# Forming the first of four weight sums of every FFN pair: an accumulating transfer from HBM issued by GpSimd in the place of a VectorE addition

## The chip, the cores and the metric

The kernel runs on one core of a Trainium2 chip. The metric is the device time of one execution in microseconds (us), lower is better. Matmul work runs on TensorE (PE), elementwise work on VectorE (DVE) and ScalarE (ACT), transfers are issued by SyncE (SP), and GpSimd (POOL) computes nothing in this kernel.

## What is computed

Two layers of a hybrid trunk, on 128 context tokens and 512 latent tokens of width 1024 (640 tokens in all), each of the form half-step SwiGLU, token mixing, half-step SwiGLU. The change touches the SwiGLU layers alone, of which there are four (`ffn_w_in` is 1024 x 5632 for each, `D_FF` is 2816):

```python
def _swiglu(h, w_in, w_out):
    g, u = jnp.split(h @ w_in, 2, axis=-1)
    return (jax.nn.silu(g) * u) @ w_out

x = x + 0.5 * mod[:, :, 2] * _swiglu(modulated(0, x), ffn_w_in[l, 0], ffn_w_out[l, 0])
...
x = x + 0.5 * mod[:, :, 8] * _swiglu(modulated(2, x), ffn_w_in[l, 1], ffn_w_out[l, 1])
```

All is float32. The kernel splits each operand in a high part (float32r, ScalarE) and a low part (the difference, VectorE) and makes each product of three matmuls: high x high, high x low, low x high.

## The kernel before, in words

**FFNs and pairs.** The four FFNs are f = 0 to 3. The hidden width of 2816 is worked off in 11 steps d = 0 to 10, each of two 128-column tiles of the gate half and two of the value half; the text calls a step a pair. Step 0 is computed plainly. Steps 1 to 10 use a scheme of seven products of half-size blocks in the place of eight: the weight block of a step is cut into a11 and a21 (input rows 0 to 511; gate columns and value columns) and a12 and a22 (input rows 512 to 1023; gate and value columns), and the seven weight operands ("items" t = 0 to 6) are these blocks or sums and differences of them. An item is 24 matmuls on PE (two parts s = 0, 1 of four k-steps and three products). Every four steps (chunks of 4, 4 and 3: after d = 3, 7 and 10) eight output units of the second weight follow, and x is updated. So steps 4 and 8 start behind output units, and step 1 behind the plain step; the others follow each other directly.

**Raw weights.** `w_raw` has two halves of 1 MB. Half 0 holds a11 and a21 of a step, half 1 holds a12 and a22. SP loads a half by two transfers of 512 KB (`load_in`, L832 to L839; `raw_in[0]` and `raw_in[1]` count the landings). It may load half 0 of step d + 1 once the low part of item 4 of step d is made (`lo_ready`) and the four sums of step d are (`sums_done`); half 1 once the low part of item 6 is. On SP's queue the loads stand between those of `w_mod` ("grains" of 512 KB), four of them ahead of or behind some steps.

**Sums.** `weight_sum(f, d, i)` (L2485) makes four operands in place in `w_raw`, on VectorE, one instruction of 128 x 1024 elements each: i = 0 is a21 = a21 + a22, and waits for both halves; i = 1 is a11 = a21 - a11, i = 2 is a12 = a12 - a11, i = 3 is a12 = a22 - a11. Item 1 is the result of i = 0, so the high part of item 1 (`item_hi`, ScalarE, L1906) waits for `sums_done`; the low part of it (`item_lo`, VectorE, L2476) waits for the high part; and PE waits for the low part (`lo_ready`). High and low parts go to a ring of four slots (`w_hi`, `w_lo`), so that item 1 of step d + 1 may be made once PE is done with item 4 of step d.

**Order.** The order on each engine is written out by hand. On VectorE, in `double(f, d)` (L2783), the first sum and the low part of item 1 of the next step stand in the middle of the step d, and between two additions of step d that PE waits for:

```python
                elif d > 1:
                    weight_sum(f, d + 1, 0)
                for s in range(2):
                    part_done(f, d, 5, s)
                    dve.wait_ge(p5_kept, done + s + 1)
                    dve.tensor_tensor(work[:, s, 2, :], work[:, s, 2, :], role(d, s, "A"), ALU.add).then_inc(c22_done, 1)
                    if not last and d > 1:
                        if s == 0:
                            item_lo(f, d + 1, 1)
```

The addition (L2815) of part s = 1 takes a bank that part s = 1 of item 6 of step d then writes: PE waits for `c22_done` at its start (`free_part`, L1081 to L1084: `t == 6`). For step 2 (`d == 1` in `double`) the first sum and the low part stand behind both additions. For step 1 the first sum stands in `sum_forms` (L2680), for steps 4 and 8 in `lead_step` (L2853), beside the output units.

On ScalarE, `double` (L2116) makes the high part of item 1 of the next step behind the two copies `keep_u2` (L2114); behind it stand two SiLUs (L2142) and the high part of item 2.

## Time and profile before

| | before |
|---|---|
| median of 3 runs | 2393.9 us (2392.03 to 2394.64) |
| the profiled execution | 2396.54 us |
| its span | 2394.7 us |
| PE busy (share of the span) | 2340.2 us (98%) |
| DVE busy | 1568.7 us (66%) |
| ACT busy | 973.1 us (41%) |
| POOL busy | 0.2 us (0%) |
| DMA queue of SP | 249.07 MB, 31.8% of 16 DMA engines' span |

The profile shows one execution. The span is the time from the first to the last instruction; the profiled execution took 1.8 us more than its span. Busy time of PE is the time covered by matmuls; what is missing to the span is idle time of PE, each piece of it put down to the instruction that ended it. A row of a group gives line, engine, operation, out<-in, count, busy time, mean time of one, and the engine's idle time just before them with its releasers. A row of a timeline gives start, duration, engine, line, operation and, in brackets, how long the engine was idle before it and what it waited for.

### The profile page before, as it was taken

How to read it: one execution, taken by the hardware profiler on the slowest of the kernel's cores; microseconds unless marked ns; L12 is line 12 of the kernel's file. 1: busy time of each engine (PE TensorE's matmuls, PEld its weight loads, DVE VectorE, ACT ScalarE, POOL GpSimd, SP SyncE). 2: the span in 40 equal slices, each digit the busy share in tenths (PEclk: the TensorE clock that was granted, in tenths of full speed). 3: DMA queues.
4: the chain of work that ended last, by engine and by line, in shares of the span. 5: the costliest groups of instructions: out<-in, count | busy, mean ns of one | idle time of the engine just before them, and what ended most of it. 6: DMA issues, size and time to landing. Idle time of an engine off the chain costs nothing.

```text
span 2394.7 us, 39770 instructions
## 1 busy us (share of the span) xinstructions
PE 2340.2 (98%) x16652; PEld 2263.6 (95%) x16652; DVE 1568.7 (66%) x2366; ACT 973.1 (41%) x1545; POOL 0.2 (0%) x4
## 2 busy tenths in 40 slices
PE   7999999999989999999999999999999999999999
PEld 6999999989769999999999999999999999999998
DVE  4886776657766876677587767676245768467463
ACT  6533423354556433414374243245215364334142
POOL 0000000000000000000000000000000000000000
PEclk9999999999999999999999999999999999999999
DMA  8342544322101252434224344333221012322132
GB/s 293 124 146 94 193 149 166 132 72 63 47 19 54 89 159 89 141 124 141 89 72 174 108 156 152 115 111 99 88 71 45 19 54 71 106 71 89 53 97 71
DMA packets 201420, 251.61 MB, mean 105 GB/s; under 512 B 12994, under 2 KB 178074, under 8 KB 201242
## 3 DMA queue, kind: packets, MB, share of 16 engines
q1 hardware_dynamic: 201242, 249.07, 31.8%
q8 instruction: 132, 2.16, 0.4%
q14 instruction: 46, 0.38, 0.1%
HBM read 245.76 MB, written 3.28 MB: 104 GB/s over the span
## 4 chain that ended last, share of the span: by engine, by line
PE 84%; DVE 6%; ACT 4%; DMA 3%; issue 3%; SPq 0%; DVEq 0%; ACTq 0%
PE banks L1052 72%; DMA w_raw<-ffn_w_in 2%; DVE w_lo L2476 2%; ACT w_hi L1906 1%; PE banks L1199 1%; DVE w_raw L2497 1%; PE banks L1390 1%; PE banks L1392 1%; PE banks L1391 1%; PE banks L1477 1%; PE banks L1489 1%; DVE hid_lo L2754 1%; ACT prob L2278 0%; PE banks L1504 0%; PE banks L1670 0%
## 5 line engine op out<-in xcount | busy, mean ns | idle before, releaser
L1052 PE MATMUL banks<-b_hi,w_hi 128*128 128x320 f32 x2496 | 779.3, 312 | 15.6 <-DVE b_lo L2654 7.9
L1052 PE MATMUL banks<-b_hi,w_lo 128*128 128x320 f32 x2496 | 772.8, 310 | 0.0
L1052 PE MATMUL banks<-b_lo,w_hi 128*128 128x320 f32 x2496 | 772.8, 310 | 0.0
L1052 PEld LDWEIGHTS banks<-b_hi,w_hi 128*128 128x128 f32 x2496 | 469.9, 188 | 35.3 <-issue 23.2
L1906 ACT ACTIVATE w_hi<-w_raw 128x1024 fp32r<-128x1024 f32 x296 | 310.3, 1055 | 416.8 <-PE banks L1052 235.9
L2476 DVE TENSOR_TENSOR w_lo<-w_raw,w_hi 128x1024 fp32r<-128x1024 f32 x296 | 361.5, 1223 | 171.7 <-ACT w_hi L1906 170.1
L1052 PEld LDWEIGHTS banks<-b_lo,w_hi 128*128 128x128 f32 x2496 | 470.1, 188 | 0.0
L1052 PEld LDWEIGHTS banks<-b_hi,w_lo 128*128 128x128 f32 x2496 | 470.0, 188 | 0.0
L1052 PE MATMUL banks<-hid_hi,w_hi 128*128 128x320 f32 x1664 | 397.0, 311 | 3.0 <-DVE hid_lo L2754 1.5
L1052 PE MATMUL banks<-hid_lo,w_hi 128*128 128x320 f32 x1664 | 394.1, 309 | 0.0
L1052 PE MATMUL banks<-hid_hi,w_lo 128*128 128x320 f32 x1664 | 394.0, 309 | 0.0
L1052 PEld LDWEIGHTS banks<-hid_hi,w_hi 128*128 128x128 f32 x1664 | 281.7, 188 | 4.8 <-DVE hid_lo L2754 2.3
L1052 PEld LDWEIGHTS banks<-hid_hi,w_lo 128*128 128x128 f32 x1664 | 282.1, 188 | 0.0
L1052 PEld LDWEIGHTS banks<-hid_lo,w_hi 128*128 128x128 f32 x1664 | 282.0, 188 | 0.0
L2504 DVE SCALAR_TENSOR_TENSOR x<-banks,mod,x 128x128 f32<-128x128 f32 x354 | 134.9, 433 | 220.9 <-PE banks L1052 220.8
L2497 DVE TENSOR_TENSOR w_raw<-w_raw 128x1024 f32<-128x1024 f32 x160 | 195.3, 1221 | 15.8 <-DMA w_raw<-ffn_w_in 10.2
L1912 ACT ACTIVATE w_hi<-w_raw 128x1024 fp32r<-128x1024 f32 (+1 forms) x96 | 93.3, 984 | 236.4 <-PE banks L1052 236.4
L2085 ACT ACTIVATE hid_hi<-work 128x640 fp32r<-128x640 f32 x88 | 64.2, 733 | 158.8 <-DVE work L2835 149.0
L2482 DVE TENSOR_TENSOR w_lo<-w_raw,w_hi 128x1024 fp32r<-128x1024 f32 (+1 forms) x96 | 107.7, 1132 | 9.8 <-ACT w_hi L1912 9.1
L1895 ACT ACTIVATE w_hi<-w_raw 128x2048 fp32r<-128x2048 f32 (+1 forms) x26 | 48.0, 1846 | 103.4 <-PE banks L1052 49.4
L2805 DVE TENSOR_TENSOR work<-work,banks 128x320 f32<-128x320 f32 x80 | 38.0, 484 | 74.3 <-ACT work L2114 74.3
L2459 DVE TENSOR_TENSOR w_lo<-w_raw,w_hi 128x2048 fp32r<-128x2048 f32 (+1 forms) x24 | 52.8, 2201 | 47.3 <-ACT w_hi L1895 47.3
(326 smaller groups left out, 2550.6 us busy)
## 6 DMA issues: line engine op xcount, KB each, us to landing
w_raw<-ffn_w_in SPq DMA_DIRECT2D x176, 512.0 KB, 4.9
mod_grain<-w_mod SPq DMA_DIRECT2D x84, 512.0 KB, 6.0
w_raw<-ffn_w_out SPq DMA_DIRECT2D x64, 512.0 KB, 4.5
last_grain<-w_mod SPq DMA_DIRECT2D x44, 512.0 KB, 6.0
w_raw<-ffn_w_out SPq DMA_DIRECT2D x32, 384.0 KB, 3.8
w_raw<-w_in_odd SPq DMA_DIRECT2D x20, 512.0 KB, 4.8
mod_first<-w_mod SPq DMA_DIRECT2D x3, 2048.0 KB, 15.8
w_raw<-w_in_even SPq DMA_DIRECT2D x12, 512.0 KB, 5.0
```

The costliest lines, as they stand in the source:

```text
L1052: ins = pe.matmul(o, w3[w], v3[v][cols], start=first and i == 0, stop=last and i == 2, skip_group_check=onto_read)
L1199: ins = pe.matmul(bank[MODB][b * MOD_ROWS:(b + 1) * MOD_ROWS, 0:KIND_COLS], wide_c[:, kt, :], by_features(grain[q])[:, b], start=kt == 0, ...
L1895: act.activation(split_view(w_hi, kind, parity(unit)), raw_view(kind, parity(unit)), ACT.Copy).then_inc(hi_ready, 1)
L1906: act.activation(ring_in(w_hi, in_slot(d, t)), operand(d, t), ACT.Copy).then_inc(hi_ready, 1)
L1912: act.activation(ring_out(w_hi, out_slot(c, u), CHUNKS[c]), out_operand(c, u), ACT.Copy).then_inc(hi_ready, 1)
L2085: act.activation(hid_hi[:, k + s, :], work[:, s, 0:2, :].rearrange("p a b -> p (a b)"), ACT.Copy)\
L2459: dve.tensor_tensor(split_view(w_lo, kind, parity(unit)), raw_view(kind, parity(unit)), split_view(w_hi, kind, parity(unit)).bitcast(F32), ...
L2476: dve.tensor_tensor(ring_in(w_lo, q), operand(d, t), ring_in(w_hi, q).bitcast(F32), ALU.subtract).then_inc(lo_ready, 1)
L2482: dve.tensor_tensor(ring_out(w_lo, q, n), out_operand(c, u), ring_out(w_hi, q, n).bitcast(F32), ALU.subtract)\
L2497: dve.tensor_tensor(out_, in0, in1, op).then_inc(sums_done, 1)
L2504: ins = dve.scalar_tensor_tensor(out=xs, in0=bank[banks[hf]][:, in_bank], scalar=mod_col(v, layer, 3 * j + 2, d), in1=xs, op0=ALU.mult, op ...
L2805: dve.tensor_tensor(work[:, s, 1, :], work[:, s, 1, :], role(d, s, "C"), ALU.add).then_inc(c12_done, 1)
```

## The change

VectorE's first sum of steps 1 to 10 of all four FFNs is gone (40 instructions). GpSimd issues in its place a transfer from HBM for each step that reads a22 from `ffn_w_in` once more (512 KB) and adds it to a21 in `w_raw`. GpSimd waits for the landing of half 0 only (`raw_in[0]`). A new semaphore, `first_weight_sum`, counts the landings; the high part of item 1 (ScalarE) and the second sum (VectorE, i = 1) wait for it.

```diff
@@ def sums_before
-            return 4 * ((DOUBLES - 1) * f + d - 1)
+            return 3 * ((DOUBLES - 1) * f + d - 1)
+
+        def first_sums_before(f, d):
+
+            return 16 * ((DOUBLES - 1) * f + d - 1)
@@ def ffn_tables
-                    loads(("in", f, d, 0), 0, in_ev(f, d, 4), sums_before(f, d) + 4)
+                    loads(("in", f, d, 0), 0, in_ev(f, d, 4), sums_before(f, d) + 3)
@@ scalar, def item_hi
+                elif t == 1:
+                    act.wait_ge(first_weight_sum, first_sums_before(f, d) + 16)
                 elif t < 6:
-                    act.wait_ge(sums_done, sums_before(f, d) + {1: 1, 3: 3, 4: 3, 5: 4}[t])
+                    act.wait_ge(sums_done, sums_before(f, d) + {3: 2, 4: 2, 5: 3}[t])
@@ gpsimd
+        @block.gpsimd
+        def _(pool):
+            w_in = a["ffn_w_in"].rearrange("l h (k p) n -> l h p k n", p=P)
+            for f in range(2 * DEPTH):
+                l, j = divmod(f, 2)
+                for d in range(1, DOUBLES):
+                    c0 = D_FF + 2 * P * d
+                    pool.wait_ge(raw_in[0], RAW_COUNT["in", f, d, 0])
+                    pool.dma_start(operand(0, 1), w_in[l, j][:, HK:KT, c0:c0 + 2 * P], accum_op=ALU.add)\
+                        .then_inc(first_weight_sum, 16)
@@ vector, def weight_sum
-                n = sums_before(f, d) + i
+                n = sums_before(f, d) + i - 1
                 a11, a21, a12, a22 = (operand(0, t) for t in range(PLAIN_ITEMS))
-                if i == 0:
-                    for h in range(2):
-                        dve.wait_ge(raw_in[h], RAW_COUNT["in", f, d, h])
+                if i == 1:
+                    dve.wait_ge(first_weight_sum, first_sums_before(f, d) + 16)
                 else:
                     dve.wait_ge(sums_done, n)
-                    dve.wait_ge(lo_ready, in_ev(f, d, (0, 2, 3)[i - 1]) + 1)
-                out_, in0, in1, op = ((a21, a21, a22, ALU.add), (a11, a21, a11, ALU.subtract), (a12, a12, a11, ALU.subtract),
-                                      (a12, a22, a11, ALU.subtract))[i]
-                dve.tensor_tensor(out_, in0, in1, op).then_inc(sums_done, 1)
+                dve.wait_ge(lo_ready, in_ev(f, d, (0, 2, 3)[i - 1]) + 1)
+                out_, in0, in1 = ((a11, a21, a11), (a12, a12, a11), (a12, a22, a11))[i - 1]
+                dve.tensor_tensor(out_, in0, in1, ALU.subtract).then_inc(sums_done, 1)
@@ vector, sum_forms (step 1), double (steps 2, 3, 5 to 7, 9, 10), lead_step (steps 4, 8)
-                weight_sum(f, 1, 0)
...
-                elif d > 1:
-                    weight_sum(f, d + 1, 0)
...
-                        weight_sum(f, d + 1, 0)
...
-                if u == 5:
-                    weight_sum(f, d, 0)
```

VectorE in the middle of step 2 of FFN 0, where item 1 of step 3 is prepared. L2805 is the second addition to `work`, L2815 the third (the one that PE waits for), L2497 a weight sum, L2476 a low part. Before:

```order
L2805 TENSOR_TENSOR work<-work,banks_7 128x320 [waits u2_kept]
L2805 TENSOR_TENSOR work<-work,banks_3 128x320 [waits u2_kept]
L2497 TENSOR_TENSOR w_raw<-w_raw 128x4x256 [waits raw_in1,raw_in0]
L2815 TENSOR_TENSOR work<-work,banks_5 128x320 [waits p5_kept,first_part]
L2476 TENSOR_TENSOR w_lo<-w_raw,w_hi 128x1024 [waits hi_ready]
L2815 TENSOR_TENSOR work<-work,banks_1 128x320 [waits p5_kept,w_used]
L2497 TENSOR_TENSOR w_raw<-w_raw 128x4x256 [waits lo_ready,sums_done]
```

The same place with the change (L2821, L2829, L2514 and L2495 are the lines L2805, L2815, L2497 and L2476 of before):

```order
L2821 TENSOR_TENSOR work<-work,banks_7 128x320 [waits u2_kept]
L2821 TENSOR_TENSOR work<-work,banks_3 128x320 [waits u2_kept]
L2829 TENSOR_TENSOR work<-work,banks_5 128x320 [waits p5_kept,first_part]
L2495 TENSOR_TENSOR w_lo<-w_raw,w_hi 128x1024 [waits hi_ready]
L2829 TENSOR_TENSOR work<-work,banks_1 128x320 [waits p5_kept,w_used]
L2514 TENSOR_TENSOR w_raw<-w_raw 128x4x256 [waits lo_ready,first_weight_sum]
```

The first sum is gone from the queue; all else keeps its place, the low part of item 1 still ahead of the second of the two additions. GpSimd's whole queue with the change:

```order
L3468 ISA
L3468 MEMSET const-float32-0.0 128x1
L3468 MEMSET const-float32-1.0 128x1
L3468 MEMSET const-bfloat16-1.0 128x1
L3468 MEMSET const-uint8-127 128x1
L2460 UNCONDITIONAL_BRANCH [waits barrier_Pool_Activation_PE_DVE_SP_gather]
L2468 DMA w_raw<-ffn_w_in 128x4x256 [waits raw_in0] x40
L67 UNCONDITIONAL_BRANCH
```

The 40 transfers are all that is new there; SP, ScalarE and PE keep their instructions in the same order, and at ScalarE the 40 high parts of item 1 wait for `first_weight_sum` where they waited for `sums_done`.

## Rows read from the trace of the kernel before

**Rows 1.** Page, part 1: busy us, share of the span, instructions of each engine.
```profile
PE 2340.2 (98%) x16652; PEld 2263.6 (95%) x16652; DVE 1568.7 (66%) x2366; ACT 973.1 (41%) x1545; POOL 0.2 (0%) x4
```
**Rows 2.** Page, part 4: the chain that ended last, by engine.
```profile
PE 84%; DVE 6%; ACT 4%; DMA 3%; issue 3%; SPq 0%; DVEq 0%; ACTq 0%
```
**Rows 3.** Page, part 5: high part, low part, weight sums.
```profile
L1906 ACT ACTIVATE w_hi<-w_raw 128x1024 fp32r<-128x1024 f32 x296 | 310.3, 1055 | 416.8 <-PE banks L1052 235.9
L2476 DVE TENSOR_TENSOR w_lo<-w_raw,w_hi 128x1024 fp32r<-128x1024 f32 x296 | 361.5, 1223 | 171.7 <-ACT w_hi L1906 170.1
...
L2497 DVE TENSOR_TENSOR w_raw<-w_raw 128x1024 f32<-128x1024 f32 x160 | 195.3, 1221 | 15.8 <-DMA w_raw<-ffn_w_in 10.2
```
**Rows 4.** PE's largest group in 64:120, 795:840, 2000:2035 (FFN 0, 1, 3, first steps).
```profile
L1052 PE MATMUL banks<-b_hi,w_hi 128*128 128x320 f32 x111 | 34.9, 314 | 2.3 <-DVE w_lo L2476 0.9 <-ACT work L2107 0.9 <-DVE work L2815 0.3
...
L1052 PE MATMUL banks<-b_hi,w_hi 128*128 128x320 f32 x96 | 30.1, 313 | 2.2 <-ACT work L2107 1.3 <-DVE work L2835 0.4 <-DVE work L2815 0.3
...
L1052 PE MATMUL banks<-b_hi,w_hi 128*128 128x320 f32 x73 | 23.0, 314 | 2.2 <-ACT work L2107 1.3 <-DVE work L2835 0.4 <-DVE work L2815 0.3
```
**Rows 5.** Timelines around item 1 of step 7 of FFN 3: DVE, ACT, PE.
```profile
2183.06 1.23 DVE L2476 TENSOR_TENSOR w_lo<-w_raw,w_hi 128x1024 fp32r<-128x1024 f32 x1 [0.73 <-ACT w_hi L1906]
2184.20 0.48 DVE L2815 TENSOR_TENSOR work<-work,banks 128x320 f32<-128x320 f32 x1
...
2181.96 1.06 ACT L1906 ACTIVATE w_hi<-w_raw 128x1024 fp32r<-128x1024 f32 x1 [1.69 <-DVE w_raw L2497]
...
2184.92 0.31 PE L1052 MATMUL banks<-b_hi,w_hi 128*128 128x320 f32 x1
```
**Rows 6.** Line L839, half 0 of that step: its two issues, landing after issue.
```profile
L839 SPq DMA_DIRECT2D w_raw<-ffn_w_in x2: 368/438/508, 2170.9 to 2171.3; - x2
...
DMA to landing us min/median/max: 4.0/4.9/5.7
```
**Rows 7.** The same of step 3 of FFN 0, and its high part of item 1.
```profile
L839 SPq DMA_DIRECT2D w_raw<-ffn_w_in x2: 378/886/1394, 104.9 to 105.3; - x2
...
DMA to landing us min/median/max: 3.8/4.8/5.8
...
116.84 1.06 ACT L1906 ACTIVATE w_hi<-w_raw 128x1024 fp32r<-128x1024 f32 x1 [4.04 <-DVE w_raw L2497]
```
**Rows 8.** The same of step 6 of FFN 0 (four grains ahead on the queue).
```profile
L839 SPq DMA_DIRECT2D w_raw<-ffn_w_in x2: 385/454/522, 238.7 to 239.1; - x2
...
DMA to landing us min/median/max: 7.3/8.1/8.9
...
252.31 1.06 ACT L1906 ACTIVATE w_hi<-w_raw 128x1024 fp32r<-128x1024 f32 x1 [2.57 <-DVE w_raw L2497]
```
**Rows 9.** The same of step 10 of FFN 3.
```profile
L839 SPq DMA_DIRECT2D w_raw<-ffn_w_in x2: 368/438/509, 2301.4 to 2301.8; - x2
...
DMA to landing us min/median/max: 4.2/4.7/5.1
...
2312.59 1.06 ACT L1906 ACTIVATE w_hi<-w_raw 128x1024 fp32r<-128x1024 f32 x1 [2.07 <-DVE w_raw L2497]
```
**Rows 10.** The same of step 2 of FFN 3 (the high parts of items 1 and 2).
```profile
L839 SPq DMA_DIRECT2D w_raw<-ffn_w_in x2: 367/438/508, 1991.2 to 1991.6; - x2
...
DMA to landing us min/median/max: 4.0/4.4/4.9
...
2003.73 2.01 ACT L1906 ACTIVATE w_hi<-w_raw 128x1024 fp32r<-128x1024 f32 x2 [4.19 <-DVE w_raw L2497]
```
**Rows 11.** Step 8 of FFN 3, behind output units: half 0 landing, high part.
```profile
L839 SPq DMA_DIRECT2D w_raw<-ffn_w_in x2: 368/442/515, 2228.0 to 2228.4; - x2
...
DMA to landing us min/median/max: 3.8/4.3/4.8
...
2256.06 1.06 ACT L1906 ACTIVATE w_hi<-w_raw 128x1024 fp32r<-128x1024 f32 x1 [8.22 <-DVE w_raw L2497]
```
**Rows 12.** All issues of line L839 (176): landing after issue.
```profile
DMA to landing us min/median/max: 3.5/4.9/14.1
```

More of the change, by code:

```diff
@@ L173, in trunk @@
         sums_done = sem("sums_done")
+        first_weight_sum = sem("first_weight_sum")
         hi_ready = sem("hi_ready")
```

## The prediction
> **What bounds the kernel now.** I read the engines' busy times first: PE is busy for 2340.2 of the 2394.7 us of the span, DVE for 66% of it, POOL for nothing [rows 1]. The chain of waits says the same of the path: 84% of it is PE's, 6% DVE's, 4% ACT's and 3% transfers' [rows 2]. So work taken from DVE is worth only what PE idles for behind it, and a wait that is added costs nothing until it outlasts what PE still has to do. The groups by line give the prices of one instruction: 1.055 us for a high part (ACT), 1.223 us for a low part and 1.221 us for a weight sum (DVE) [rows 3]. The 40 sums that go are 40 x 1.221 = 48.8 us of DVE's time.
>
> Where does PE wait behind DVE inside the FFNs? In the first steps of FFN 0, 1 and 3 its largest group idled for 2.3, 2.2 and 2.2 us, 6.7 us in all, behind low parts, the addition L2815 and copies that come late because DVE has run late [rows 4]. That is what an emptier DVE can win at most; I found no other such waits of size.
>
> **How tight the order is.** The timelines around item 1 of step 7 of FFN 3 show it. ACT makes the high part of item 1 from 2181.96, having idled for the first sum; DVE makes the low part from 2183.06; only then comes the second addition L2815, from 2184.20 to 2184.68; and PE starts the matmul of item 6 that needs it at 2184.92 [rows 5]. So here the high part of item 1 can start 2184.92 - 2184.68 = 0.24 us later and no more. The low part itself isn't due at PE for another 6 us; what is due is the addition queued behind it on DVE. In the other steps that follow each other directly this reserve is 0.05 to 0.3 us (the same reading; 1.1 in one).
>
> Until now the first sum had to wait for half 1. With the change it waits for half 0 alone, which lands earlier. In that step the later of its two transfers was issued at 2171.3 and landed 5.7 us later, at 2177.0 [rows 6]. So if **X** is the time from the landing of half 0 to the landing of the accumulating transfer, X may be 2181.96 - 2177.0 + 0.24 = 5.2 us before PE waits. I call this the room of a step.
>
> **The rooms of all 40.** The same sum gives 116.84 - 111.1 = 5.7 us, with the reserve 5.8, for step 3 of FFN 0, the first of this kind [rows 7]; 252.31 - 248.0 + 0.3 = 4.6 for its step 6, the smallest, where grains of the modulation stand ahead of half 0 on SP's queue and delay its landing to 8.9 us [rows 8]; and 2312.59 - 2306.9 = 5.7 for step 10 of FFN 3, the last [rows 9]. Read like this, the 24 steps that follow a step of the main scheme give:
> - FFN 0, steps 3, 5, 6, 7, 9, 10: 5.8, 9.6, 4.6, 5.6, 9.9, 5.4
> - FFN 1: 5.0, 9.1, 7.3, 8.1, 9.6, 6.8
> - FFN 2: 4.8, 9.6, 6.4, 8.1, 9.7, 6.1
> - FFN 3: 4.8, 8.2, 5.8, 5.2, 8.4, 5.7
>
> Step 2 is another kind: both additions stand ahead of the low part, but DVE's chain already makes PE late there, so each us of delay counts at once. Its room is 2003.73 - 1996.5 = 7.2 us in FFN 3 [rows 10], as much in FFN 0 and 1; in FFN 2 PE did not wait, and it is 9.8. The 12 steps 1, 4 and 8 lie behind plain or output products: in step 8 of FFN 3 half 0 landed at 2233.2 and the high part began at 2256.06, 22.9 us later [rows 11]; the smallest of the 12 rooms is 19 us. I cost these at nothing; output units or the plain step hide them, and they would begin to cost from an X of 19 us on.
>
> **The price of X.** No accumulating transfer and nothing issued by POOL is in this trace. From below the nearest row is the fastest of the 176 plain transfers of this size from this tensor, 3.5 us from issue to landing; from above, the slowest, 14.1 us, which had stood in a queue [rows 12]. An addition in place must fetch two operands of 512 KB where a plain load fetches one. Where two transfers of a half went through a queue without grains ahead, the first took 3.8 to 4.2 us [rows 6, 7, 9 to 11]; 3.9, near the middle of them, doubled is **7.8 us**, which I take. It is my largest choice. It leaves out that half 1 or grains often travel at the same time, which lengthens it, and that the fixed part of a transfer needn't double, which shortens it.
>
> The Trainium skill (DMA: Bandwidth & Descriptors, Anatomy of one DMA) puts a transfer issued by GpSimd at about 2.0 us and its bytes at 436 GB/s, which makes 3.2 us of 512 KB; an estimate from that page alone is below every room, and the sum would then have only the gain of the first rival. It is for plain transfers; no run here shows one from GpSimd. Against the change speaks another page of the Trainium skill (Collectives: The Full Stack, The bandwidth ceiling: the fold count and why AG ≠ RS ≠ AR): an addition inside a transfer needs two reads for one write and pushes twice the read traffic. The rows can't show that yet; 7.8 is what it would be if the whole of 3.9 doubled.
>
> **The sum.** A step whose room is smaller than X makes PE wait for the difference, once. The waits add up: after one, everything that releases the next load of half 0 (low part of item 4, behind DVE's chain) has moved by as much as PE has. At X = 7.8 us, 14 of the 24 steps are short: FFN 0 2.0 + 3.2 + 2.2 + 2.4 = 9.8, FFN 1 2.8 + 0.5 + 1.0 = 4.3, FFN 2 3.0 + 1.4 + 1.7 = 6.1, FFN 3 3.0 + 2.0 + 2.6 + 2.1 = 9.7, together 29.9 us. Three steps 2 are short by 0.6: 1.8 us. In step 1 of FFN 0 DVE is 1.2 us ahead, which takes away the 0.9 us that PE waits there for a low part [rows 4]. The second high part, the SiLUs and the second sum queue behind the late high part on ACT and DVE, but they are late by the same amount as PE; nothing more. The 40 sums off DVE are otherwise worth nothing: PE's work hides them. Half 1 shares the DMA engines with 40 x 0.52 = 21 MB more; it landed before the first sum began, and item 2 is made some 2 us after item 1, so I cost its delay at nothing, and up to 10 us in all if the reserve runs out in single steps.
> Sum: 29.9 + 1.8 - 0.9 = **+31 us**. Against the profiled execution's own 2396.5 that is 2427.5; that execution stands 2.6 us above the median of the runs, so 2393.9 + 31 = **2425 us**.
>
> **Rivals**, by X; all at the same place, ACT's high part of item 1, except the last.
> - *Faster: DVE's relief decides.* At X of 5.3 us or less five steps at most are short, 2.1 us in all, and DVE's chain in the first steps starts up to 2 us earlier, so that the 6.7 us of PE's waits [rows 4] go. At X = 4.9 (the usual landing of a plain transfer [rows 12]) it is 0.5 - 6.7 = -6 us: 2388. For it speaks that a fixed part doesn't double; against it that two operands are moved, and that half 1 leaves at about the same time. Chance 0.10.
> - *Hidden, no change:* X from 5.3 to 6.4. At 6, ten steps cost 7.3 us, relief gives back some 5: 2396. Chance 0.15.
> - *The forecast:* X from 6.4 to 9.5, from 12 to 66 us more. Chance 0.40.
> - *Twice a transfer in traffic:* the usual 4.9 us [rows 12] doubled is 9.8, or more if POOL is slow to issue. Then 27 of the 28 steps are short, 74 us: 2468; at 12 us it is 135, at 14.1 it is 194: 2588. For it speaks that half 1 and four grains of 512 KB are on the engines in many steps, and that a plain half 0 behind grains landed after 8.9 us [rows 8]. Chance 0.30.
> - *Something else sets the end:* the added traffic slows half 1 and the grains, so that item 2 or the modulation products come late. Up to 10 us on top of any case, and some 5 by itself: 2399. Chance 0.05, mostly slower.
>
> **How the numbers follow.** The likeliest case is the third; its own range is 2406 to 2460. The range reaches from 2388 (half of the first rival is left out, 0.05) to 2393.9 + 135 = 2529 for X = 12 (beyond it I leave 0.12). A measurement of this kernel tells 0.2%, 4.8 us, from no change. Faster by more: 0.10. Within: 0.15 + 0.02. Slower by more: the rest, 0.73.
>
> **What would show it.** POOL or the transfers' list has 40 issues with X as their time to landing, near 7.8 us. ACT's line of the high part idles for that transfer and no longer for the weight sum. PE waits for the addition L2829 (L2815 before) in steps with small rooms, 2 to 3 us each, in FFN 0 and 3 most, and in none of steps 1, 4, 8. DVE's weight sums are 120, its busy time 49 us less. It is wrong if PE's new waits stand elsewhere, if steps with rooms above 9 us wait while X is below 9, or if the waits of the steps don't add up to the difference.

## The result and the profile after

| | before | changed |
|---|---|---|
| median, same series | 2393.76 us (4 runs) | 2470.75 us (2468.41 to 2475.15, 4 runs) |
| ratio to before | | 1.032, 95% interval 1.0307 to 1.0333 |
| span of the profiled execution | 2394.7 us | 2467.8 us |
| PE busy | 2340.2 us | 2357.3 us |
| span less PE busy | 54.5 us | 110.5 us |

The change makes the kernel 77 us slower, where +31 was forecast: the direction and the range hold, the size doesn't. Of the 73 us between the two spans, 56 are idle time of PE and 17 are matmuls that took longer. The page and PE's waits, of the changed kernel; L1057, L2829, L2495, L2514 and L1913 are L1052, L2815, L2476, L2497 and L1906 of before. The line `q0` is GpSimd's queue (packets, MB, share of the DMA engines), the line behind it the chain that ended last. In the waits: us in total, times, longest us:

```profile
PE 2357.3 (96%) x16652; PEld 2280.4 (92%) x16652; DVE 1525.9 (62%) x2326; ACT 974.7 (39%) x1545; POOL 51.7 (2%) x44
...
q0 software_dynamic: 21120, 20.97, 5.6%
...
PE 71%; DMA 12%; DVE 6%; ACT 5%; issue 5%; SPq 0%; DVEq 0%; POOL 0%; ACTq 0%; POOLq 0%
...
L1057 PE MATMUL banks<-b_hi,w_hi 128*128 128x320 f32 x2496 | 787.4, 315 | 72.6 <-DVE work L2829 51.8
...
L2514 DVE TENSOR_TENSOR w_raw<-w_raw 128x1024 f32<-128x1024 f32 x120 | 146.6, 1221 | 5.4
```
```profile
PE banks L1057 <- DVE work L2829: 51.8, 14, 8.3
PE banks L1057 <- DVE b_lo L2671: 7.9, 5, 2.7
...
PE banks L1057 <- DVE w_lo L2495: 4.9, 1, 4.9
PE banks L1057 <- ACT work L2114: 3.9, 3, 1.3
```

The weight sums are 120 now and took 146.6 us against 195.3 [rows 3]. DVE's busy time fell by 42.8 us, and the kernel gained nothing by it [rows 1]. The chain has 12% of transfers where it had 3% [rows 2]. PE waits 51.8 us, in 14 pieces of up to 8.3 us, for the addition behind the low part of item 1, and once, 4.9 us, for the low part itself (step 2 of FFN 2, where both additions stand ahead of it). Before, it waited for the addition for 1.6 us in 6 pieces:

```profile
PE banks L1052 <- DVE work L2815: 1.6, 6, 0.3
```

The line of the new transfer, of the same trace (issue time of GpSimd, who waited, landing after the start of the issue):

```profile
L2468 POOL DMA_DIRECT2D w_raw<-ffn_w_in x40: 1282/1282/1425, 42.2 to 2378.3; - x40
...
  ACT w_hi L1913: 119.3, 20
DMA to landing us min/median/max: 5.7/6.9/13.4
```

X is the time from the landing of half 0 to the landing of this transfer. Read from the trace, it is 6.0 us at least, 7.1 in the middle and 13.9 at most over all 40, and 7.7 in the middle over the 28 steps without 1, 4 and 8. At step 7 of FFN 3, the one of [rows 5], X and the place of the wait came as forecast; ACT, DVE and PE there, of the changed kernel:

```profile
2252.33 1.06 ACT L1913 ACTIVATE w_hi<-w_raw 128x1024 fp32r<-128x1024 f32 x1 [3.96 <-DMA w_raw<-ffn_w_in]
...
2253.42 1.22 DVE L2495 TENSOR_TENSOR w_lo<-w_raw,w_hi 128x1024 fp32r<-128x1024 f32 x1 [3.24 <-ACT w_hi L1913]
2254.56 0.48 DVE L2829 TENSOR_TENSOR work<-work,banks 128x320 f32<-128x320 f32 x1
...
2255.10 0.41 PE L1057 MATMUL banks<-b_hi,w_hi 128*128 128x320 f32 x1 [1.92 <-DVE work L2829]
```

X is 7.8 us here against a room of 5.2; PE waits 1.9, where 2.6 was forecast, and the granted clock is then at half from 2256.6 to 2260.0. Step 6 of FFN 1 is what the forecast didn't have. SP, POOL, ACT, DVE and PE there:

```profile
971.95 6.66 SPq L844 DMA_DIRECT2D w_raw<-ffn_w_in  x4
978.65 1.65 SPq L864 DMA_DIRECT2D mod_grain<-w_mod  x3
980.34 0.71 SPq L864 DMA_DIRECT2D last_grain<-w_mod  x1
...
978.01 1.30 POOL L2468 DMA_DIRECT2D w_raw<-ffn_w_in  x1 [27.48 <-DMA w_raw<-ffn_w_in]
...
991.46 1.06 ACT L1913 ACTIVATE w_hi<-w_raw 128x1024 fp32r<-128x1024 f32 x1 [8.64 <-DMA w_raw<-ffn_w_in]
...
992.55 1.22 DVE L2495 TENSOR_TENSOR w_lo<-w_raw,w_hi 128x1024 fp32r<-128x1024 f32 x1 [7.92 <-ACT w_hi L1913]
993.69 0.48 DVE L2829 TENSOR_TENSOR work<-work,banks 128x320 f32<-128x320 f32 x1
...
994.22 0.64 PE L1057 MATMUL banks<-b_hi,w_hi 128*128 128x320 f32 x1 [6.60 <-DVE work L2829]
994.66 0.47 PE L1057 MATMUL banks<-b_lo,w_hi 128*128 128x320 f32 x1
...
997.37 0.31 PE L1057 MATMUL banks<-b_hi,w_hi 128*128 128x320 f32 x1
```

From 978.65 on SP issues four grains of 512 KB behind half 1. The adding transfer, issued at 978.01, lets ACT start at 991.46, 13.4 us later, and PE waits 6.60 us, not at item 1 but at the addition queued on DVE behind it. The matmuls behind the wait take 0.47 us in the place of 0.31 until 997. The windows of PE around that place (PE busy and instructions, granted clock, DMA share, GB/s) show the clock at half, its level of 1.2 GHz, in those 3 us:

```profile
984.00:994.00 10.00, 3.62 (x25) 0.81 0.72 208
994.00:997.00 3.00, 2.78 (x10) 0.50 0.00 0
997.00:1000.00 3.00, 3.00 (x21) 0.99 0.00 0
```

Over the whole trace the granted clock was 0.5 for 84 us, where it was 29 us before.

**The rooms against the measured X.** I take the rooms of the prediction and the X of each step from this trace. The shortfalls come to 65.5 us over the 28 steps. Measured from the end of item 1 of a step back to the end of item 1 of the step before it, the 28 steps are 75.0 us longer. Step by step the two go together, but for the four steps 2:

| step (FFN, step) | room | X | short by | longer by |
|---|---|---|---|---|
| 0, 6 | 4.6 | 10.7 | 6.1 | 7.8 |
| 1, 3 | 5.0 | 10.3 | 5.3 | 8.0 |
| 1, 6 | 7.3 | 13.9 | 6.6 | 7.1 |
| 1, 10 | 6.8 | 12.5 | 5.7 | 6.3 |
| 2, 2 | 9.8 | 12.7 | 2.9 | 6.5 |
| 2, 3 | 4.8 | 12.6 | 7.8 | 10.6 |
| 2, 6 | 6.4 | 13.4 | 7.0 | 8.5 |
| 2, 10 | 6.1 | 13.4 | 7.3 | 7.8 |
| the other 20 | 4.8 to 9.9 | 6.0 to 9.3 | 16.7 in all | 12.4 in all |

Step 2 of FFN 0, 1 and 3 is short by 1.9 to 2.1 us and only 0.3 to 0.9 longer, step 2 of FFN 2 short by 2.9 and 6.5 longer. Eight steps with an X over 10 us hold 49 of the 65.5 us. What sets them apart is when SP issues the first of the next two to four grains, counted from the landing of half 0. In the eight it is from 0.8 us before it to 1.5 us after it (1.2 in the example above, which has an X of 13.9). In step 2 of FFN 0 it is 1.7 us after, with an X of 9.3. In the other 11 with grains it is 2.2 to 4.2 us after, and X is 6.0 to 6.7. In the eight without any grain X is 6.3 to 9.2. So the number of grains alone isn't it (step 5 of FFN 2 has four of them, with an X of 6.2); they must get in beside the transfer while it has most of its way ahead. Half 1 counts as well. In the eight steps without a grain X is 9.1 and 9.2 where SP issues half 1 0.5 and 0.7 us after the landing of half 0 (step 2 of FFN 3 and 1), and 6.3 where it does so 2.0 us before it (step 3 of FFN 3). The steps with rooms above X (steps 5 and 9 of every FFN, step 7 of FFN 1 and 2) are longer by -0.4 to 0.0.

### The profile page after: what moved, and what is told of

It reads as the page before. It is cut to its first block, busy times and chain, and to the rows that moved or that the text cites. A ratio compares the mean times of both kernels' runs of the same rounds, so it can differ in the third digit from the quotient of the medians.

```text
span 2467.8 us, 39730 instructions
## 1 busy us (share of the span) xinstructions
PE 2357.3 (96%) x16652; PEld 2280.4 (92%) x16652; DVE 1525.9 (62%) x2326; ACT 974.7 (39%) x1545; POOL 51.7 (2%) x44
## 3 DMA queue, kind: packets, MB, share of 16 engines
q0 software_dynamic: 21120, 20.97, 5.6%
## 4 chain that ended last, share of the span: by engine, by line
PE 71%; DMA 12%; DVE 6%; ACT 5%; issue 5%; SPq 0%; DVEq 0%; POOL 0%; ACTq 0%; POOLq 0%
PE banks L1057 60%; DMA w_raw<-ffn_w_in 12%; ACT w_hi L1913 2%; DVE w_lo L2495 2%; PE banks L1395 1%; PE banks L1397 1%; PE banks L1396 1%; PE banks L1482 1%; PE banks L1494 1%; DVE w_raw L2514 1%; DVE hid_lo L2770 1%; PE banks L1204 1%; ACT prob L2285 0%; PE banks L1509 0%; PE banks L1675 0%
## 5 line engine op out<-in xcount | busy, mean ns | idle before, releaser
L1057 PE MATMUL banks<-b_hi,w_hi 128*128 128x320 f32 x2496 | 787.4, 315 | 72.6 <-DVE work L2829 51.8
L1057 PE MATMUL banks<-b_lo,w_hi 128*128 128x320 f32 x2496 | 779.6, 312 | 0.0
L1057 PE MATMUL banks<-b_hi,w_lo 128*128 128x320 f32 x2496 | 779.3, 312 | 0.0
L1057 PEld LDWEIGHTS banks<-b_hi,w_hi 128*128 128x128 f32 x2496 | 476.4, 191 | 92.7 <-DVE work L2829 55.5
L2495 DVE TENSOR_TENSOR w_lo<-w_raw,w_hi 128x1024 fp32r<-128x1024 f32 x296 | 361.8, 1224 | 244.3 <-ACT w_hi L1913 242.0
L1913 ACT ACTIVATE w_hi<-w_raw 128x1024 fp32r<-128x1024 f32 x296 | 310.0, 1055 | 483.9 <-PE banks L1057 327.4
L1057 PEld LDWEIGHTS banks<-b_lo,w_hi 128*128 128x128 f32 x2496 | 476.9, 191 | 0.0
L1057 PEld LDWEIGHTS banks<-b_hi,w_lo 128*128 128x128 f32 x2496 | 476.2, 191 | 0.0
L1057 PE MATMUL banks<-hid_hi,w_hi 128*128 128x320 f32 x1664 | 397.9, 311 | 3.0 <-DVE hid_lo L2770 1.5
L1057 PE MATMUL banks<-hid_lo,w_hi 128*128 128x320 f32 x1664 | 394.5, 309 | 0.0
L1057 PE MATMUL banks<-hid_hi,w_lo 128*128 128x320 f32 x1664 | 394.5, 309 | 0.0
L1057 PEld LDWEIGHTS banks<-hid_hi,w_hi 128*128 128x128 f32 x1664 | 282.2, 188 | 4.8 <-DVE hid_lo L2770 2.3
L1057 PEld LDWEIGHTS banks<-hid_lo,w_hi 128*128 128x128 f32 x1664 | 282.8, 188 | 0.0
L1057 PEld LDWEIGHTS banks<-hid_hi,w_lo 128*128 128x128 f32 x1664 | 282.4, 188 | 0.0
L2514 DVE TENSOR_TENSOR w_raw<-w_raw 128x1024 f32<-128x1024 f32 x120 | 146.6, 1221 | 5.4
L2468 POOL DMA_DIRECT2D w_raw<-ffn_w_in x40 | 51.5, 1288 | 2327.7 <-DMA w_raw<-ffn_w_in 2327.7
L2821 DVE TENSOR_TENSOR work<-work,banks 128x320 f32<-128x320 f32 x80 | 38.1, 485 | 78.1 <-ACT work L2121 78.1
```

The lines of the kernel that those rows point to most:

```text
L1057: ins = pe.matmul(o, w3[w], v3[v][cols], start=first and i == 0, stop=last and i == 2, skip_group_check=onto_read)
L1913: act.activation(ring_in(w_hi, in_slot(d, t)), operand(d, t), ACT.Copy).then_inc(hi_ready, 1)
L2468: pool.dma_start(operand(0, 1), w_in[l, j][:, HK:KT, c0:c0 + 2 * P], accum_op=ALU.add)\
L2495: dve.tensor_tensor(ring_in(w_lo, q), operand(d, t), ring_in(w_hi, q).bitcast(F32), ALU.subtract).then_inc(lo_ready, 1)
L2514: dve.tensor_tensor(out_, in0, in1, ALU.subtract).then_inc(sums_done, 1)
L2821: dve.tensor_tensor(work[:, s, 1, :], work[:, s, 1, :], role(d, s, "C"), ALU.add).then_inc(c12_done, 1)
```

## The experiments

Twelve kernels ran, each beside the kernel before on the same chip, whose median was 2396.5 us in the series of the first four, 2395.1 in that of the next four and 2394.0 in that of the last four. Their differences to it, each in its own series (e4 and e5 are the names that some of the expectations use):

| kernel | us | to before |
|---|---|---|
| the change | 2470.75 | +77.0 |
| grains held back | 2431.25 | +34.8 |
| plain copy (one run) | 2401.87 | +5.4 |
| a quarter of the bytes (one run) | 2395.06 | -1.4 |
| additions ahead of the low part (e4) | 2440.29 | +43.8 |
| the same, SiLUs ahead of the high part (e5) | 2441.73 | +46.6 |
| both orders, no transfer | 2391.82 | -3.3 |
| transfer in steps 1, 4, 8 only | 2391.43 | -3.7 |
| PE kept busy in seven waits | 2479.05 | +83.9 |
| grains held back and both orders | 2396.66 | +2.7 |
| steps 1, 4, 8 and both orders | 2388.69 | -5.3 |
| few long waits, no transfer | 2460.29 | +66.3 |
| many short waits, no transfer | 2461.93 | +68.0 |

### Grains held back until the transfer has landed

```diff
@@ SP, ahead of the grains behind half 1 (both places)
+                        sp.wait_ge(first_weight_sum, first_sums_before(f, d) + 16)
                         load_grain(added, 0)
...
+                            sp.wait_ge(first_weight_sum, first_sums_before(f, d + 1) + 16)
                             load_window(f, where)
```

> Against the changed kernel (2470.8 us), SP holds the modulation grains that it would issue right behind half 1 until the accumulating transfer has landed; nothing else differs. Theory A (the accumulating transfer takes 6.0 to 6.5 us by itself and 10 to 14 us where two or four grains of 512 KB share the engines with it): the eight landings above 10 us fall to 6 to 8.5 us, their shortfalls against the rooms from 49 us to some 12 us, and with the slower clock behind the long waits gone too the time is 2415 to 2430 us. Theory B (the transfer is slow by itself in those steps, or POOL is late to issue): X stays at 10 to 14 us in them and the time at 2470 us or more, since the grains come later.

2431.25 us (2424.74 to 2432.83, 4 runs), ratio 1.0141 (1.0122 to 1.016). PE's waits, and the landing of the 40 transfers, in this kernel's trace:

```profile
PE banks L1059 <- DVE work L2831: 27.5, 16, 3.4
```
```profile
DMA to landing us min/median/max: 5.8/6.6/9.9
```

With nothing moved but the time at which SP issues the grains, 42 of the 77 us are gone, the longest wait at the addition is 3.4 us in the place of 8.3, and the slowest landing 9.9 in the place of 13.4. So the grains beside the transfer cost over half of the result. In the eight steps X fell from 10.3 to 13.9 us to 6.3 to 10.4. What is left, +35, is close to the +31 of the forecast, but not for its reason alone: half 1 still travels beside the transfer. In this trace X is 8.5 to 10.4 us in the nine of the 28 steps in which half 1 is issued between 0.3 us before and 0.9 us after the landing of half 0, and 6.1 to 6.8 in the six in which it is issued 2.0 us after it or later, with no grain beside the transfer in either. The time came out 1 us above the range of theory A.

### A plain copy in the place of the addition

```diff
-pool.dma_start(operand(0, 1), w_in[l, j][:, HK:KT, c0:c0 + 2 * P], accum_op=ALU.add)\
+pool.dma_start(operand(0, 1), w_in[l, j][:, HK:KT, c0:c0 + 2 * P])\
```

> The 40 transfers from POOL are plain copies of the same 512 KB into the same place (a21 is overwritten by a22 instead of added to; item 1 and what follows from it are computed from a22 alone). Theory A1 (adding costs, since two operands are fetched): X without grains falls from 6.2 us to 4.5 us or less, and the time to 2440 us or less. Theory A2 (the path through POOL costs: issue of 1.28 us, its descriptors, and sharing with half 1): X stays within 0.5 us of the changed kernel's, and so does the time, within 10 us.

2401.87 us in one run. This kernel leaves the addition out, so item 1 is a22 alone. The transfer's line and landing, and PE's wait:

```profile
L2468 POOL DMA_DIRECT2D w_raw<-ffn_w_in x40: 748/748/882, 42.5 to 2311.2; - x40
...
DMA to landing us min/median/max: 3.8/4.8/8.1
```
```profile
PE banks L1057 <- DVE work L2829: 9.8, 5, 4.0
```

The same bytes from HBM, not added, land 2.1 us earlier in the middle (4.8 against 6.9) and GpSimd issues in 0.75 us against 1.28. The whole landing spread moves down with it: the slowest is 8.1 in the place of 13.4, and it too belongs to a step with four grains beside it. So a room of 5 to 10 us is enough for a copy in most steps and isn't for an addition.

### A quarter of the bytes

```diff
-pool.dma_start(operand(0, 1), w_in[l, j][:, HK:KT, c0:c0 + 2 * P], accum_op=ALU.add)\
+pool.dma_start(operand(0, 1)[:, 0:1, :], w_in[l, j][:, HK:HK + 1, c0:c0 + 2 * P], accum_op=ALU.add)\
```

> Each accumulating transfer moves and adds 128 KB (the first of four input blocks) instead of 512 KB; three quarters of the first sum are left out. If X is a fixed part and a part by size, X without grains is 6.2 us minus three quarters of the part by size: with 1.5 to 3 us for 512 KB it is 4 to 5 us; if nearly all is fixed it stays above 5.5 us. With X near 4.5 us, below every room, the room theory expects no wait of PE behind the addition and a time of 2388 to 2394 us. If PE's waits have another cause (added traffic, GpSimd and VectorE sharing a port), half or more of the 77 us stay.

2395.06 us in one run, against 2396.5 of before (2393.8 to 2398.1, 7 runs): no difference can be told. This kernel leaves three quarters of the first sum out. Its transfer and PE's wait:

```profile
L2468 POOL DMA_DIRECT2D w_raw<-ffn_w_in x40: 862/862/1005, 42.6 to 2304.7; - x40
...
DMA to landing us min/median/max: 3.0/3.8/8.0
```
```profile
PE banks L1057 <- DVE work L2829: 7.5, 3, 4.0
```

X was 3.3 us at least for 128 KB and 6.0 for 512 KB. A straight line through both gives 2.4 us that don't depend on the size and 3.6 for 512 KB. X is 4.1 us in the middle here, but up to 8.3 in steps with grains beside the transfer, so that three waits at the addition stay, where none was expected. All but eight of the 28 steps are covered and five of these miss by 0.4 us at most, and the relief that the prediction's first rival spoke of shows: PE waits 0.9 us for the copies L2114 against 3.5 for the same line of before (L2107), and its waits of 0.9 each for a low part and for the last products are gone [rows 4]. That is 4.4 of the 6.7 us. The three waits that are left at the addition, 7.5 us, outweigh it, and the time stays where it was.

### The additions ahead of the low part, on VectorE

```diff
@@ double, VectorE
                     dve.tensor_tensor(work[:, s, 2, :], work[:, s, 2, :], role(d, s, "A"), ALU.add).then_inc(c22_done, 1)
-                    if not last and d > 1:
-                        if s == 0:
-                            item_lo(f, d + 1, 1)
-                        else:
-                            weight_sum(f, d + 1, 1)
...
-                    if d == 1:
-                        item_lo(f, d + 1, 1)
-                        weight_sum(f, d + 1, 1)
+                    item_lo(f, d + 1, 1)
+                    weight_sum(f, d + 1, 1)
```

> The changed kernel with VectorE's second addition of part 5 moved ahead of the low part of item 1 (steps 3, 5 to 7, 9, 10). Room theory (PE waits for the addition because it is queued behind the low part, not for the weights of item 1, which are due 6 us later): the rooms grow by 5.8 us to 10.4 to 15 us, some 14 us of shortfall stay (four steps 2 and the steps with X above 12), the waits of PE for the addition go from 52 us to near 0, and the time is 2400 to 2415 us. If PE needed item 1 itself, the wait moves to the low part L2495 and the time stays within 10 us of 2471.

2440.29 us (2437.47 to 2440.8), ratio 1.0182 (1.0166 to 1.0197): 33 us won, where the expectation had 56 to 71. PE's waits:

```profile
PE banks L1057 <- DVE w_lo L2495: 15.7, 10, 5.2
PE banks L1057 <- ACT work L2114: 15.1, 11, 2.7
```

No wait for the addition is left, so the order was the place where X came through. But the waits went on to the next two users: the low part itself (15.7 us) and the copies L2114 of the step after (15.1), which stand on ACT behind the late high part. X stayed as it was (7.2 in the middle, 13.9 at most), with ten of them over 10 us. In steps 6 and 10 of FFN 1 and 2 an X of 12.8 to 13.9 us made the step only 0.4 to 1.7 us longer, so there the rooms had grown by 5 to 6 us, as expected. Most of what was left is in other steps: 7.8 us in step 2 of FFN 2 and 3.4 in that of FFN 0, whose order this edit doesn't change, 5.2 in step 6 of FFN 0 and 3.5 and 3.0 in step 7 of FFN 1 and 2, where X had grown to 10.3 and 9.8.

### The SiLUs ahead of the high part as well, on ScalarE

```diff
@@ double, ScalarE
-                elif d > 1:
-                    item_hi(f, d + 1, 1)
...
-                if d == 1:
+                if not last:
                     item_hi(f, d + 1, 1)
```

> The kernel e4 (2440.3 us) with one more reordering: on ScalarE the two SiLUs of a step stand ahead of the high part of the next item 1, so that they no longer queue behind the accumulating transfer. In e4 PE's waits had become low parts (15.7 us), the copy L2114 (15.1 us) and the last products (6.8 us). Theory C (these come from the SiLUs and what follows them queueing behind the late high part): they fall by half or more and the time is 2415 to 2430 us. Theory D (they come from item 1's own low part and from VectorE's chain behind it, which is the same in both): within 6 us of e4.

2441.73 us (2429.47 to 2448.35), ratio 1.0188 (1.0156 to 1.0219), no different from the kernel above. PE waited 17.1 us for L2114 and 14.7 for the low part. The two SiLUs behind the high part weren't what held PE.

### Both orders in the kernel before

The two diffs above, made in the kernel before.

> The kernel before with both reorderings of e5 and nothing else; it tells how much of e4's and e5's time is the reordering's own. The reserve of 0.05 to 0.3 us at the addition goes up by about 1.2 us there, but VectorE's and ScalarE's later work moves later by the same. Expected: 2390 to 2397 us, no change (at most 3 us are to be had, PE's small waits for the addition). If the reordering itself costs PE waits, 2400 us or more, and e4 and e5 understate what it gives beside the transfer.

2391.82 us (2387.65 to 2394.51, 10 runs), ratio 0.9984 (0.9975 to 0.9994). The orders alone are worth 3.3 us, so most of the 33 and 30 us of the two kernels above are room given to the transfer and not a gain of their own.

### The transfer in steps 1, 4 and 8 only

```diff
-                for d in range(1, DOUBLES):
+        LEADS = (1, 4, 8)
+                for d in LEADS:
...
@@ VectorE, double: in the other steps as before
+                elif d > 1:
+                    weight_sum(f, d + 1, 0)
```

> The transfer makes the first sum in steps 1, 4 and 8 of every FFN only (12 transfers, rooms of 19 us and more); in the other 28 VectorE makes it as in the kernel before. Room theory: nothing waits, whatever X is up to 19 us; the time is that of the kernel before, 2392 to 2397 us, perhaps 1 us less for the wait at step 1 of FFN 0. If accumulating transfers cost by themselves (6.3 MB more traffic, GpSimd's issue, VectorE slowed), 12/40 of the 77 us, some 23 us, would be seen.

2391.43 us (2387.8 to 2393.14, 10 runs), ratio 0.9985 (0.9976 to 0.9995). Its transfers, with nobody in the list of who waited for them:

```profile
L2477 POOL DMA_DIRECT2D w_raw<-ffn_w_in x12: 1282/1282/1425, 42.4 to 2228.6; - x12
...
DMA to landing us min/median/max: 5.8/6.0/9.3
```

The 12 steps that the prediction put at nothing, for rooms of 19 us and more, cost nothing, and the 12 sums taken from DVE win 3.7 us: PE's waits of 0.9 us each for a low part and for the last products [rows 4] are gone, and that for the copies fell from 3.5 to 2.4. All 77 us come from the other 28 steps.

### PE kept busy in the longest waits

```diff
@@ TensorE, item 6, s == 1, in 7 steps, ahead of the wait for the addition
+                        for _ in range(30):
+                            pe.matmul(bank[7][:, 0:HALF], ring_in(w_hi, q)[:, 3, 0:P], b_hi[:, 6, 3, :], start=True, stop=True)
                     pe.wait_ge(c22_done, n)
```

> The changed kernel; in the seven longest of PE's waits for the addition (5 to 8 us each, behind the first part of item 6 of steps FFN 0: 5, FFN 1: 2, 5, 9, FFN 2: 2, 5, 9) PE first runs 30 matmuls whose result nobody uses (30 x 0.147 = 4.4 us at the full clock), so that it is not idle for all of the wait. Clock theory: in the changed kernel the granted clock fell to half for 3.4 to 10 us after such waits, 84 us in all against 29 before; PE's busy time rose by 17 us through it. With PE busy in the wait the half-clock time falls to 35 to 55 us and the time from 2471 to 2452 to 2465 us. If the clock costs nothing beside the wait (the transfer decides alone), 2469 to 2473 us; if the dummy work is in the way, more.

2479.05 us (2475.3 to 2489.04), ratio 1.0356 (1.033 to 1.0382): 7 us more against before than the changed kernel, and not 6 to 19 less as the clock theory asked for. PE's busy time, with 210 matmuls more than before, and its wait:

```profile
PE 2385.7 (96%) x16862; PEld 2307.5 (93%) x16862; DVE 1525.3 (62%) x2326; ACT 973.5 (39%) x1545; POOL 51.7 (2%) x44
```
```profile
PE banks L1057 <- DVE work L2833: 33.4, 15, 5.1
```

The clock was at half for 63 us against 84. PE was busy for 28 us more than in the changed kernel, but 32 of its busy us are the added matmuls; all others together took 3.5 us less, in line with the clock. The added matmuls should have filled idle time, and PE's idle time fell by 16 us only. In six of the seven places PE still waited behind them, 0.2 to 3.5 us, so they were hardly in the way there. What grew is X, by 0.7 us in the mean of the 28 steps. The phase of the steps against the grains moved as well: step 7 of FFN 1 had an X of 6.0 in the changed kernel and 11.3 in this one. This run doesn't isolate the clock, and I don't count it for or against the clock theory.

### Both measures on the changed kernel: grains held, both orders

> The changed kernel with the modulation grains held back until the accumulating transfer has landed, and with both additions to work ahead of the low part of item 1 (VectorE) and the two SiLUs and copies ahead of the high part (ScalarE). Theory (the cost is the room of a step less X, and X is longest behind grains): the two measures act on different terms, X down to a median of 7 and rooms up, so the time is below either alone: 2408 to 2422 us, PE's waits behind the chain of item 1 under 25 us in all and none above 3 us. Rival (what the order gives is only moved to the waits for the low part and for the SiLU copies, as the reordered kernels showed with 15 us each): 2425 to 2432, as with the held grains alone.

2396.66 us (2392.83 to 2401.22, 11 runs), ratio 1.0013 (1.0004 to 1.0022), below what I expected. PE's waits behind the chain of item 1, and the landings:

```profile
PE banks L1059 <- ACT work L2116: 7.3, 7, 1.3
...
PE banks L1059 <- DVE work L2842: 3.2, 3, 1.3
```
```profile
DMA to landing us min/median/max: 5.6/6.2/8.7
```

The held grains alone won 42 us and the orders alone 33 (the first of them) or 30 (both); together they won 74. They act on the two sides of the same difference, X and the room. This is the strongest evidence for the account by rooms: the transfer is still there 40 times, with all its bytes, X is 9.0 us at most, and 74 of the 77 us are gone. Against the orders alone (-3.3) the transfer still costs 6 us.

### The best of the parts: transfer in steps 1, 4 and 8, both orders

> The accumulating transfer in steps 1, 4 and 8 only, VectorE's sum in the others, and both reorderings of the kernel before. The two edits gave 2391.4 and 2391.8 us each by itself, where the kernel before had 2395.1. Theory: they take away different waits (the first the late low parts in the first steps of an FFN, the second the waits for the addition in the middle), so together 2387 to 2390. Rival: both shorten the same small waits of 5 to 7 us, so together 2390 to 2392, no better than one.

2388.69 us (2387.09 to 2391.92, 11 runs), ratio 0.998 (0.9972 to 0.9989). It is the fastest of all, 5.3 us below the kernel before; the two gains of 3.3 and 3.7 add up in part.

### Waits made on purpose: few and long, many and short

In the kernel before, with no transfer added, the low part of item 1 is written again n times before the addition that PE waits for, n = 6 in 7 steps or n = 2 in 21:

```diff
@@ item_lo, VectorE
+                if t == 1 and (f, d) in steps:
+                    for i in range(n):
+                        dve.tensor_tensor(ring_in(w_lo, q), operand(d, t), ring_in(w_hi, q).bitcast(F32), ALU.subtract).then_inc(again, 1)
+                        dve.wait_ge(again, n * steps.index((f, d)) + i + 1)
```

> The kernel before, with the low part of item 1 written six more times in 7 steps (3 and 7 of the FFNs, without step 7 of FFN 3), each behind the one before: 42 extra instructions of VectorE, which hold back the addition that PE waits for by 6 x 1.3 = 7.8 us in each of the 7 steps. The waits alone come to 7 x 7.6 = 53 us. Clock theory (a wait of this length is followed by a stretch of matmuls at the granted clock of 0.5, and such stretches cost about as much again as half their length): PE's busy time rises by 12 to 20 us, total 2395 + 53 + 12 to 20 = 2460 to 2468. Rival (the clock costs nothing of its own, the stretches at half clock would be there anyway): 2448 and PE's busy time within 3 us of before.

> The same 42 extra instructions of VectorE in the kernel before, but two each in 21 steps, so that PE waits 2 x 1.3 - 0.2 = 2.4 us 21 times, 50 us in all. Clock theory: waits this short leave the clock as it is, PE's busy time within 3 us of before, total 2445, 15 to 25 us under the kernel with the few long waits. Rival (only the sum of the waits counts): both kernels within 3 us of each other.

2460.29 us (2457.47 to 2464.33) with the few long waits, 2461.93 (2460.16 to 2464.7) with the many short ones. PE's busy time and its wait, first of the few long ones, then of the many short ones:

```profile
PE 2357.3 (96%) x16652; PEld 2281.5 (93%) x16652; DVE 1621.1 (66%) x2408; ACT 973.7 (40%) x1545; POOL 0.2 (0%) x4
```
```profile
PE banks L1053 <- DVE work L2821: 52.9, 12, 7.8
```
```profile
PE 2362.1 (96%) x16652; PEld 2282.9 (93%) x16652; DVE 1620.7 (66%) x2408; ACT 974.5 (40%) x1545; POOL 0.2 (0%) x4
```
```profile
PE banks L1053 <- DVE work L2821: 47.7, 23, 2.8
```

In both, waits of 53 and 48 us made the kernel 66 and 68 us longer, and PE busy for 17 and 22 us more with the same matmuls. So added waits do bring slower matmuls with them, which the clock theory said; but short waits bring as much as long ones, which it denied. The granted clock was at half for 92 us with the long waits and for 69 with the short ones (29 before). Of these PE was busy for 63 and 62 us, against 22 before: with the long waits more of the time at half clock falls into the wait itself. At half the clock, half of the additional 41 and 40 us is lost, an estimate of 21 and 20 us beside the 17 and 22 measured. For the changed kernel it is 57 us against 22, an estimate of 18 beside the 17 measured. So the slower matmuls are those at half clock. In the second kernel a wait of 2.78 us ends at 848.09 and the granted clock is at half for the next 6 us (PE, PEld, DVE, ACT, POOL busy, then the clock):

```profile
848.00:851.00 3.00, 2.91 (x11) 2.91 (x12) 2.90 (x4) 0.00 (x0) 0.00 (x0) 0.50 0.00 0
851.00:854.00 3.00, 3.00 (x13) 3.00 (x12) 2.92 (x6) 1.53 (x2) 0.00 (x0) 0.50 0.00 0
```

Another of 2.79 us, at 402 us, and one of 2.18 at 230 weren't followed by it; of the 18 waits of 2.2 to 2.8 us 11 were.

## Why the prediction was wrong in size and right in kind

**The mechanism held.** PE waits at the addition behind the low part of item 1, on DVE, in the steps that follow each other; steps 1, 4 and 8 wait for nothing; the 49 us of sums taken from DVE are worth little by themselves (4.4 us of PE's waits where X is short). The kernels with the other orders showed the place, the one with the transfer in steps 1, 4 and 8 the steps. No step with a room above its X got longer, so the rooms read from the trace of before held on that side. On the other side those of the steps 2 didn't: there "each us of delay counts at once" gave 1.9 to 2.1 us for FFN 0, 1 and 3 at the measured X, and the steps were 0.3 to 0.9 longer; in FFN 2 it gave 2.9, and the step was 6.5 longer. The waits were not in FFN 0 and 3 most, as forecast, but in FFN 1 and 2, with 38 of the 52 us. The prediction's last sign of being wrong came true: the waits of the steps don't add up to the difference (PE's idle time grew by 56 us, the span by 73).

**The step that failed is the price of X, taken as one 7.8 us for all steps.** The prediction said that this "leaves out that half 1 or grains often travel at the same time". As a middle value it was good (measured 7.7 over the 28 steps), as a value for every step it wasn't: from 6.0 to 13.9. A room turns X into a cost only where X is larger, so the spread costs, not the mean. In the eight steps with an X over 10 the rooms at 7.8 us give 13.6 us, and the shortfalls are 48.8; in all others it is 18.1 against 16.7. The missing 35 us of waits are in the eight. That the grains make most of them is shown by holding the grains back, which took 42 us off; half 1 issued beside the transfer lengthens it too, to between 8.5 and 10.4 us without any grain. The prediction had put the traffic's cost at nothing, or at 10 us, because it asked what the transfer does to half 1 and to the grains, and not what they do to the transfer. Its fourth rival, "twice a transfer in traffic", had the cause, with the price put on all steps alike; 74 us, its first value, came near the result for a wrong reason (at its 9.8 us the listed rooms leave 26 of the 28 steps short, not 27; the sum of 74 stands).

**The term that was missing is the slower matmuls.** PE was busy for 17 us more. The prediction counted a wait at its length. The two kernels with waits made on purpose have 65 and 66 us more of span for 48 and 44 us more of idle time, factors of 1.35 and 1.5; the changed kernel has 73 for 56, a factor of 1.3, and the one with the grains held back 34 for 28, 1.2. Had the 31 us been multiplied by 1.3, the forecast had been some 40.

**The reason given for X was half right.** 7.8 was 3.9 doubled, for an addition that fetches two operands. Against the plain copy the addition costs 1.9 us at the least landing (5.7 against 3.8) and 2.1 in the middle. GpSimd's issue is 0.5 us longer; how much of that is in the landing isn't shown. Doubling overstated it; the traffic made up for it. The Trainium skill (Collectives: The Full Stack, The bandwidth ceiling: the fold count and why AG ≠ RS ≠ AR) says of a collective that it is the two reads of the addition that make it slower than a copy; the trace agrees in the direction, with 5.7 against 3.8 us. That the reads are the cause here isn't shown: the adding transfer also went in 3.7 times as many packets (21120 against 5760), and the two weren't tried apart. The Trainium skill (DMA: Bandwidth & Descriptors, Anatomy of one DMA) gave the estimate of 3.2 us for a plain transfer of this size; the copy from GpSimd took 3.8 us at the fastest, and the addition 5.7, so that estimate would have misled here. The Trainium skill (DMA: Bandwidth & Descriptors, Queues, rings and completion order) says that an engine serves the queues that have work for it in turn. The landing of 13.4 us beside half 1 and four grains, and 9.9 at most with the grains held back, agree with it; that the turns are what makes it wasn't tried by itself.

**Open** stays which of the 17 us belongs to which wait, and why some short waits are followed by half clock and others of the same length aren't. The factor of 1.2 to 1.5 is measured on sums of waits and not on one wait.

## What to carry to other kernels

A transfer that takes over an elementwise operation takes its place in a chain, so ask first what stands queued behind the reader of its result, and how much later that may come in each step. Then price the transfer by step and in the traffic that its issue meets, not by one value: the steps in which other loads leave at the same moment decide, and moving those loads may be worth more than anything else. Use it where the room is above the longest landing that the traffic can make of it (here rooms of 19 us and more with an X of 9.6 at most cost nothing), and count a new wait of the bounding engine at more than its length (1.2 to 1.5 times here).

## What the runs showed of the hardware

- An adding transfer of 512 KB from HBM, issued by GpSimd, landed after 5.7 us at the least and held GpSimd for 1.28 us; a plain one after 3.8 us, for 0.75 us. Its packets were 21120 against 5760 for the same 20.97 MB.
- In step 5 of FFN 2 half 1 was issued 2.9 us and the first of four grains 4.0 us after half 0 had landed, and X was 6.2 us; in step 6 it was 0.1 us before and 0.9 us after it, and X was 13.4. With the grains held back X was 8.5 in step 6. SP's `mod_grain` transfers took 6.7 us in the middle (6.0 before), and 4.6 when they were issued only after its landing.
- In the changed kernel PE's granted clock was at half around or behind each of the eight waits of 4.8 to 8.3 us, and behind two of 1.9 and 2.0 us; with many short waits, behind 11 of 18 of 2.2 to 2.8 us. Waits of 53 us, 51 of them in 7 places, made PE 17 us more busy; waits of 48 us, spread over 21 steps, 22 us.
